# Three reorderings around the attention chains of a two-block transformer kernel on one Trainium2 core

## The chip, the core and the metric

The kernel runs on one core of one Trainium2 chip. The metric is the device time of one execution in microseconds (us). Before the change three executions took 1301.56, 1304.0 and 1314.62 us; the median is 1304.0 us. TensorE (PE) does the matmuls, VectorE (DVE) and ScalarE (ACT) work between them on PSUM and SBUF, GpSimd (POOL) makes one half of each split weight, and SyncE (SP) issues the weight stream.

## The reference, cut to what matters

All inputs are float32, the sequence has 256 tokens and the model width is 1024. A first block has windowed attention and a bidirectional mLSTM, a gated merge and a convolutional feed-forward layer. A second model of two layers follows: its first mixer has eight "forgetting" heads (fox) and eight "stick-breaking" heads (sb), its second a short convolution, and each is followed by a feed-forward layer. The fox heads and the output product are what most of the change is about:

```python
def forgetting_attention(q, k, v, log_f):
    cum_f = jnp.cumsum(log_f, axis=-1)
    ...
        logits = jnp.einsum('bhqd,bhkd->bhqk', qi, k,
                            preferred_element_type=jnp.float32) * scale
        logits = logits + fi[..., :, None] - cum_f[:, :, None, :]
        logits = jnp.where(causal, logits, -jnp.inf)
        p = jax.nn.softmax(logits, axis=-1)
        return jnp.einsum('bhqk,bhkd->bhqd', p.astype(v.dtype), v)
...
    o = jnp.concatenate([o_fox, o_sb], axis=1)
    o = o.transpose(0, 2, 1, 3).reshape(b, s, MIX_WIDTH)
    return o @ w_out
```

The other place is the first block's attention, where the gate `gm` is one of the input projections and the softmax runs over latent keys, context keys and a sink.

## The kernel before

**Weights.** Every 128x1024 weight block is loaded by SP into `raw`, rounded by ACT into `whi` (line 1146, `splits_upto`), and the remainder is made by POOL into `wlo` (line 313). A product is three matmuls, high by high, high by low and low by high (lines 482 to 484, `mm3`). The three buffers are rings of six blocks, so a block's ACT split waits until the block six places earlier has been used up (`blk_done`).

**Order.** Each engine has one hand-written program. Nothing is scheduled by a planner; the order of the Python loops is the order on the engine, and semaphores tie the engines together.

**First attention.** TensorE goes through 16 steps `st`. A step has the scores (`att_scores`, lines 770 and 774), in eight of the steps one `gm` projection of 24 matmuls (`gp_job`, steps 1, 3, 5, 7, 9, 11, 15 and 16, from the table `GM_AT`), the transposes of the step before (`att_transposes`, line 785), and in odd steps the values and reciprocals of a pair (`att_values` line 796, `att_recips` line 807). All `gm` projections write the same PSUM bank, so each of them waits until ACT has evacuated the one before (`evac`, line 1238, which also makes the next weight's split). On ACT a step is: `evac` of the projection of step `st - 1`, then the two exponentials of step `st` (lines 1325 and 1327), then in even steps the copy of the reciprocals (line 1334), for which a DVE multiply waits (line 1895).

**Fox chain.** For head h the chain is

- `fox_scores(h)` on TensorE: eight matmuls, lines 1010 to 1016, into one of two banks
- `fox_maximum(h)` on DVE: two reductions, line 2120
- `fox_exps(h)` on ACT: two exponentials, line 1468
- `fox_even(h)` on DVE: reciprocal and two scalings, lines 2126 and 2129
- `fox_transposes(h)` on TensorE: three transposes, line 1028, which wait for `fox_even(h)`
- `fox_turned(h)` on DVE: copy out of PSUM, line 2137
- `fox_values(b)` on TensorE for two heads: lines 1037 and 1041 (the sb heads have `sb_values`, lines 988 and 992)
- `out_hi`, `out_lo` on ACT (line 1459) and DVE (line 2113): the split of the pair's output for the last product

`scores(h)` waits for the exponentials of head h - 2, since there are two score banks. On TensorE iteration h holds `fox_transposes(h - 2)`, `fox_scores(h)`, in the first two iterations `sb_values(3)` and the products that spread the norms (`spread_rstd`, line 924), for h from 4 to 7 one half of an output product (`out_half(h - 4, 0)`, twelve matmuls of lines 482 to 484), and for even h from 4 a `fox_values`.

The output product of eight blocks accumulates in eight PSUM regions. For blocks 0 to 3 it is cut into two halves, `out_half(n, 0)` for the first four regions and `out_half(n, 1)` for the rest. A first half may start as soon as the norms of all queries and keys are done, a second one only when all fox exponentials are done, because its banks hold the scores. Blocks 4 and 5 (`product_k`) and the pair 6 and 7 follow whole.

On DVE the last pass of the projection loop (`j == 17`) and the lines behind it are `fox_maximum(0)`, `finish_qk(10)`, `sb_exponents(7)`, `fox_even(0)`, `sb_masked(7)`, `finish_qk(11)`, `row_rstd(3)` (four short operations, lines 1578 to 1582), `fox_maximum(1)`. After that iteration h is `fox_turned(h - 2)`, `fox_even(h - 1)`, `fox_maximum(h)`, with h = 2 as an exception that puts the maximum first. On ACT pass 17 is `fox_exps(0)`, `row_rsqrt(3)` (lines 1432 and 1435), `sb_weights(7)` (line 1454), `out_hi(2)`.

Of the kernel before, what the change touches and what calls it, by code (L numbers as in the profile page):

```python
# [36 lines left out]
GM0 = W_IN_JOBS.index("gm")  # L37
# [88 lines left out]
def build(nc, xc_d, ccol_d, params_d, const_d, const1_d, const2_d, wgate_d, wf_d, stream_d, out_d):  # L126
# [3 lines left out]
    with ctx:  # L130
# [349 lines left out]
        def _(pe):  # L480
# [565 lines left out]
            def out_half(n, half):  # L1046

                wait_rest(pe, S_OUT2 + n)
                pe.wait_ge(S["t2_lo"], n + 1)
                if half == 0:  # L1050
                    pe.wait_ge(S["qk_fin"], 26)
                else:
                    pe.wait_ge(S["fox_exp"], 16)
                for m in range(4 * half, 4 * half + 4):
                    mm = mm3(PS[:, m // 2, (m % 2) * T:(m % 2) * T + T], *w(S_OUT2 + n, m), *out_rows(n),
                             n == 0 and m % 2 == 0, False)
                if half == 1:
                    mm.then_inc(blk_done, 1)
# [24 lines left out]
            for h in range(2, 11):  # L1083
                if h < 10:
                    fox_transposes(h - 2)
                if h < 8:
                    fox_scores(h)
                if h == 2:
                    sb_values(3)
                if h in (2, 3):  # L1090
                    spread_rstd(2 * h + 8)
                    spread_rstd(2 * h + 9)
                if 4 <= h < 8:
                    out_half(h - 4, 0)
                if h in (8, 9):
                    out_half(h - 8, 1)
                if h in (4, 6, 8, 10):
                    fox_values((h - 4) // 2)
            for n in (2, 3):
                out_half(n, 1)  # L1100
            for n in (4, 5):
                wait_rest(pe, S_OUT2 + n)
# [30 lines left out]
        def _(act):  # L1133
# [180 lines left out]


            for st in range(STEPS + 3):
                if st - 1 in GM_AT:
                    evac(GM0 + GM_AT[st - 1])
                if st < STEPS:
                    for half in range(2):  # L1320
                        u = 2 * st + half
                        act.wait_ge(S["att_max"], u + 1)
                        if u >= 4:
                            act.wait_ge(S["tr_done"], u - 3)
                        act.activation(a_P[u % 4], PS[:, SCORE_BANKS[st % 2][half], :], ACT.Exp, bias=nmx[:, u:u + 1],
                                       accum_out=rsum[:, u:u + 1]).then_inc(S["att_exp"], 1)
                        act.activation(esk[:, u:u + 1], nmx[:, u:u + 1], ACT.Exp, bias=pr("sink", u, u + 1))\
                           .then_inc(S["sink_act"], 1)
                if st % 2 == 0 and st >= 4:
                    b = (st - 4) // 2  # L1330
                    act.wait_ge(S["recip_bc"], b + 1)
                    if b >= 1:
                        act.wait_ge(S["att_out"], b)
                    act.activation(a_R, PS[:, 6, T:2 * T], ACT.Copy).then_inc(S["recip_out"], 1)
# [116 lines left out]
            def sb_weights(h):  # L1451

                act.wait_ge(S["sb_arg"], h + 1)
                act.activation(sbW[h % 4], sbW[h % 4], ACT.Exp).then_inc(S["sb_w"], 1)
# [16 lines left out]
            for j in range(18):  # L1471
                if j == 17:
                    fox_exps(0)
                if j in (5, 9, 13, 17):
                    g = (j - 5) // 4
                    if g >= 1:
                        act.wait_ge(S["rq_done"], 2 + g)
                    row_rsqrt(g)
                if j == 17:
                    sb_weights(7)  # L1480
                if 0 <= j - 9 < 8:
                    sb_logs(j - 9)
                if 0 <= j - 10 < 7:
                    sb_weights(j - 10)
                if j in (13, 15, 17):
                    out_hi((j - 13) // 2)
                if j < 16:
                    act.wait_ge(blk_done, S_ATT2 + KC + j + 1)
                    if 6 <= j < 14:
                        act.wait_ge(S["fin_bc"], j - 5)  # L1490
                    if j >= 2:
                        act.wait_ge(S["st_done"], 10 + j - 1)
                    act.activation(sqr2[j % 2], PS[:, 4 + j % 2, 0:T], ACT.Square).then_inc(S["qk_sq"], 1)
                    if j == 4:
                        act.wait_ge(S["f_add"], 1)
                        act.activation(fr[1][0:8, :], fr[0][0:8, :], ACT.Abs).then_inc(S["f_act"], 1)
                        act.wait_ge(S["f_act"], 1)
                        act.activation(fr[1][0:8, :], fr[1][0:8, :], ACT.Exp, scale=-1.0).then_inc(S["f_act"], 1)
                        act.wait_ge(S["f_act"], 2)
                        act.activation(fr[1][0:8, :], fr[1][0:8, :], ACT.Ln, bias=1.0).then_inc(S["f_act"], 1)  # L1500
                    splits_upto(S_ATT2 + KC + j + RING)
# [40 lines left out]
        def _(dve):  # L1542
# [600 lines left out]
            for j in range(18):  # L2143
                if j in (5, 9, 13):
                    row_rstd((j - 5) // 4)
                if j == 6:
                    forget_sums()
                if j == 17:
                    fox_maximum(0)
                if 7 <= j:  # L2150
                    finish_qk(j - 7)
                if 0 <= j - 10 < 8:
                    sb_exponents(j - 10)
                if 0 <= j - 9 < 8:
                    sb_terms(j - 9)
                if j == 17:
                    fox_even(0)
                if 0 <= j - 10 < 8:
                    sb_masked(j - 10)
                if j in (13, 15):  # L2160
                    out_lo((j - 13) // 2)
                if j < 16:
                    dve.wait_ge(S["qk_sq"], 10 + j + 1)
                    dve.tensor_copy(q2[:, j, :], PS[:, 4 + j % 2, 0:T]).then_inc(S["evac_v"], 1)
                if j == 3:
                    dve.wait_ge(S["gates2_ps"], 1)
                    dve.tensor_scalar(fr[0][0:8, :], PS[0:8, 7, 0:T], pr("fb", rows=slice(0, 8)), None, ALU.add)\
                       .then_inc(S["f_add"], 1)
# [1 line left out]

            finish_qk(11)
            row_rstd(3)
            fox_maximum(1)
            for h in range(2, 12):
                if h < 10:
                    fox_turned(h - 2)
                if h == 2:
                    fox_maximum(h)
                    out_lo(2)
                if h < 9:  # L2180
                    fox_even(h - 1)
                if 3 <= h < 8:
                    fox_maximum(h)
                if h in (2, 3):
                    finish_qk(2 * h + 8)
                    finish_qk(2 * h + 9)
# [209 lines left out]
```

## Time and profile before

| | us |
|---|---|
| median of three executions | 1304.0 (1301.56 to 1314.62) |
| the profiled execution | 1304.0 |
| its span, first to last instruction | 1302.2 |
| TensorE busy in it | 1256.8 |
| mean granted TensorE clock | 0.984 of full speed |

The page gives one execution. Its busy times say how long an engine had work in flight; its chain says what ended last; its timeline gives the start and the duration of every instruction. Matmuls are pipelined, so a row's duration is longer than the distance to the next row's start, and the distance is what the engine's time costs. The granted clock is given for any stretch: 1.00 is 2.4 GHz and 0.50 is 1.2 GHz.

### The profile page before, as it was taken

To read this page: it belongs to the slowest core of one execution; us is meant where nothing else is said; L and a number is where in the kernel's file an instruction comes from. 1 tells how busy PE (TensorE), PEld (TensorE's weight loads), DVE (VectorE), ACT (ScalarE), POOL (GpSimd) and SP (SyncE) were. 2 spreads that over 40 slices of the span, in tenths; PEclk is the share of its full clock that TensorE was granted. 3 is DMA by queue.
4 is the path that set the end of the run, shared out by engine and by line. 5 is a ranking of instruction groups with operands and counts; after the bars stand their busy time and mean duration, and the time that the engine had idled before them with its cause. 6 is when DMAs were issued, how large, how long until landed. Compare 5 with 4: busy or idle time off the path is not lost.

```text
span 1302.2 us, 24847 instructions
## 1 busy us (share of the span) xinstructions
PE 1256.8 (97%) x9248; PEld 1150.0 (88%) x9248; DVE 784.6 (60%) x1432; ACT 628.6 (48%) x1081; POOL 700.2 (54%) x299
## 2 busy tenths in 40 slices
PE   5789999999999899999899999999999999999998
PEld 1578888877799799999888778999999999999998
DVE  3699467536631477766555663677776424677775
ACT  3523233445443555555544543655455545645553
POOL 1546563252148555557585312655566886755564
PEclk9899999999999899999999989999999999999999
DMA  9568662141125445545453211455446555445552
GB/s 376 205 218 304 222 210 68 63 129 51 49 91 167 132 147 192 193 174 215 154 178 114 82 49 51 144 194 186 171 176 211 164 186 169 156 169 192 193 188 72
DMA packets 57739, 208.45 MB, mean 160 GB/s; under 512 B 6576, under 2 KB 7600, under 8 KB 57408
## 3 DMA queue, kind: packets, MB, share of 16 engines
q1 hardware_dynamic: 57168, 205.55, 46.2%
q0 software_dynamic: 496, 1.87, 0.4%
q8 instruction: 50, 0.82, 0.3%
q14 instruction: 25, 0.20, 0.1%
HBM read 206.35 MB, written 1.05 MB: 159 GB/s over the span
## 4 chain that ended last, share of the span: by engine, by line
PE 89%; DVE 6%; DMA 3%; issue 1%; ACT 1%; SPq 0%; DVEq 0%; ACTq 0%
PE ps L482 24%; PE ps L483 23%; PE ps L484 23%; DMA raw<-in_stream 3%; PE ps L703 2%; PE ps L517 2%; PE ps L519 2%; PE ps L520 2%; PE ps L547 1%; PE ps L770 1%; PE ps L796 1%; PE ps L785 1%; DVE raw L1647 1%; PE ps L924 1%; PE ps L1016 1%
## 5 line engine op out<-in xcount | busy, mean ns | idle before, releaser
L313 POOL TENSOR_TENSOR wlo<-raw,whi 128x1024 fp32r<-128x1024 f32 x286 | 694.4, 2444 | 564.0 <-ACT whi L1146 539.6
L482 PE MATMUL ps<-Hh,whi 128*128 128x256 f32 (+2 forms) x1976 | 578.2, 293 | 15.8 <-DVE Hl L1613 4.7
L483 PE MATMUL ps<-Hl,whi 128*128 128x256 f32 (+2 forms) x1976 | 569.1, 288 | 0.0
L484 PE MATMUL ps<-Hh,wlo 128*128 128x256 f32 (+2 forms) x1976 | 568.8, 288 | 0.0
L482 PEld LDWEIGHTS ps<-Hh,whi 128*128 128x128 f32 (+1 forms) x1976 | 382.2, 193 | 30.2 <-issue 16.6
L1146 ACT ACTIVATE whi<-raw 128x1024 fp32r<-128x1024 f32 x338 | 352.9, 1052 | 111.7 <-DMA raw<-in_stream 56.1
L483 PEld LDWEIGHTS ps<-Hl,whi 128*128 128x128 f32 (+1 forms) x1976 | 382.8, 194 | 3.0
L484 PEld LDWEIGHTS ps<-Hh,wlo 128*128 128x128 f32 (+1 forms) x1976 | 382.5, 194 | 2.6
L2002 DVE SCALAR_TENSOR_TENSOR arena<-ps,sm,arena 128x255 f32<-128x255 f32 (+1 forms) x264 | 127.3, 482 | 102.7 <-ACT arena L1396 94.8
L482 PE MATMUL ps<-dh,whi 128*128 128x256 f32 x592 | 167.7, 283 | 1.5 <-DVE dl L1914 1.1
L483 PE MATMUL ps<-dl,whi 128*128 128x256 f32 x592 | 167.5, 283 | 0.0
L484 PE MATMUL ps<-dh,wlo 128*128 128x256 f32 x592 | 167.5, 283 | 0.0
L1396 ACT ACTIVATE arena<-ps,sm 128x256 f32<-128x256 f32 x132 | 66.5, 504 | 133.2 <-DVE ps L1992 104.3
L482 PEld LDWEIGHTS ps<-dh,whi 128*128 128x128 f32 x592 | 113.6, 192 | 1.9 <-issue 1.3
L484 PEld LDWEIGHTS ps<-dh,wlo 128*128 128x128 f32 x592 | 113.7, 192 | 0.0
L483 PEld LDWEIGHTS ps<-dl,whi 128*128 128x128 f32 x592 | 113.7, 192 | 0.0
L1964 DVE COPY sm<-params 128x8 f32 (+1 forms) x66 | 89.9, 1367 | 7.9 <-DVE arena L2002 7.6
L1975 DVE TENSOR_TENSOR wlo<-raw,whi 128x1024 fp32r<-128x1024 f32 x52 | 81.2, 1562 | 1.5
L1407 ACT ACTIVATE dh<-ps 128x256 fp32r<-128x256 f32 x60 | 23.0, 384 | 101.3 <-DVE ps L2011 101.3
L1647 DVE SCALAR_TENSOR_TENSOR raw<-raw,arena 128x1024 f32<-128x1024 f32 x32 | 56.4, 1792 | 4.4 <-DMA raw<-in_stream 4.2
L517 PE MATMUL ps<-whi,Hh 128*128 128x512 f32 (+1 forms) x128 | 48.0, 375 | 4.0 <-DVE Hl L1634 4.0
L519 PE MATMUL ps<-whi,Hl 128*128 128x512 f32 (+1 forms) x128 | 47.5, 371 | 0.0
(298 smaller groups left out, 1230.1 us busy)
## 6 DMA issues: line engine op xcount, KB each, us to landing
raw<-in_stream SPq DMA_DIRECT2D x386, 512.0 KB, 4.1
X<-in_xc SPq DMA_DIRECT2D x2, 1024.0 KB, 10.1
out_y<-X SPq DMA_DIRECT2D x8, 128.0 KB, 2.0
kx<-in_const POOLq DMA_DIRECT2D x1, 512.0 KB, 6.9
arena<-in_wgate POOLq DMA_DIRECT2D x1, 400.0 KB, 8.8
params<-in_params POOLq DMA_DIRECT2D x1, 372.0 KB, 6.8
k<-in_const POOLq DMA_DIRECT2D x1, 256.0 KB, 4.5
kx<-in_const POOLq DMA_DIRECT2D x1, 256.0 KB, 4.5
```

The costliest lines, as they stand in the source:

```text
L313: pool.tensor_tensor(wlo[:, slot, :], raw[:, rslot, :], whi[:, slot, :].bitcast(f32), ALU.subtract).then_inc(rest_done[0], 1)
L482: pe.matmul(out, lh, rh, start=start, stop=False, skip_group_check=True)
L483: pe.matmul(out, lh, rl, start=False, stop=False, skip_group_check=True)
L484: return pe.matmul(out, ll, rh, start=False, stop=stop, skip_group_check=True)
L517: pe.matmul(out, Hh[:, k, tok], wh_, start=k == 0 and first, stop=False, skip_group_check=True)
L519: pe.matmul(out, Hl[:, k, tok], wh_, start=False, stop=False, skip_group_check=True)
L1146: act.activation(whi[:, s % RING, :], raw[:, r % RING, :], ACT.Copy).then_inc(hi_done, 1)
L1396: act.activation(tc, PS[:, 4 + 2 * slot + j, 0:T], ACT.Identity, bias=bias, scale=cwb[:, slot, 3 * j:3 * j + 1]).then_inc(S["centre"], 1)
L1647: dve.scalar_tensor_tensor(raw[:, r % RING, :], raw[:, r % RING, :], 1.0, c_across, ALU.mult, ALU.mult, accum_out=MODB[:, at:at + 1]).then ...
L1964: dve.tensor_copy(cwb[:, i % 2, :], src).then_inc(S["cw_copy"], 1)
L1975: dve.tensor_tensor(wlo[:, s % RING, :], raw[:, RAW_OF_W[s] % RING, :], whi[:, s % RING, :].bitcast(f32), ALU.subtract).then_inc(rest_done ...
L2002: dve.scalar_tensor_tensor(tc[:, lo:hi], u[:, src:src + hi - lo], cwb[:, slot, 3 * j + 1 + n:3 * j + 2 + n], tc[:, lo:hi], ALU.mult, ALU.a ...
```

## The change

It has four parts, and no arithmetic changes.

1. First attention, ACT: `evac` of a `gm` projection moves from before the exponentials of the next step to behind them.
2. Projection loop, pass 17: on ACT `sb_weights(7)` moves ahead of `row_rsqrt(3)`. On DVE `fox_even(0)` leaves this pass, and `out_lo(2)` enters it at its end.
3. Fox loop on DVE: it now starts at h = 1, and the maximum of head h stands ahead of `fox_even(h - 1)` in every iteration; `fox_even(0)` comes behind `fox_maximum(1)`.
4. Fox loop on TensorE: the four `out_half(n, 0)` leave iterations 4 to 7. Two of them stand in iteration 8 and two in iteration 9, and all four `out_half(n, 1)` follow the loop. A first half now waits for the split outputs of all four sb pairs (`t2_lo` of 4).

```diff
                 wait_rest(pe, S_OUT2 + n)
-                pe.wait_ge(S["t2_lo"], n + 1)
                 if half == 0:
+                    pe.wait_ge(S["t2_lo"], 4)
                     pe.wait_ge(S["qk_fin"], 26)
...
-                if 4 <= h < 8:
-                    out_half(h - 4, 0)
                 if h in (8, 9):
-                    out_half(h - 8, 1)
+                    out_half(2 * h - 16, 0)
+                    out_half(2 * h - 15, 0)
                 if h in (4, 6, 8, 10):
                     fox_values((h - 4) // 2)
-            for n in (2, 3):
+            for n in range(4):
                 out_half(n, 1)
...
             for st in range(STEPS + 3):
-                if st - 1 in GM_AT:
-                    evac(GM0 + GM_AT[st - 1])
                 if st < STEPS:
...
+                if st - 1 in GM_AT:
+                    evac(GM0 + GM_AT[st - 1])
...
                 if j == 17:
                     fox_exps(0)
+                    sb_weights(7)
...
                     row_rsqrt(g)
-                if j == 17:
-                    sb_weights(7)
...
-                if j == 17:
-                    fox_even(0)
                 if 0 <= j - 10 < 8:
                     sb_masked(j - 10)
-                if j in (13, 15):
+                if j in (13, 15, 17):
                     out_lo((j - 13) // 2)
...
-            fox_maximum(1)
-            for h in range(2, 12):
-                if h < 10:
+            for h in range(1, 12):
+                if 2 <= h < 10:
                     fox_turned(h - 2)
-                if h == 2:
+                if h < 8:
                     fox_maximum(h)
-                    out_lo(2)
-                if h < 9:
+                if 1 <= h < 9:
                     fox_even(h - 1)
-                if 3 <= h < 8:
-                    fox_maximum(h)
```

**ACT in the first attention.** Before, from the exponentials of an odd step (lines 1325 and 1327) over the evacuation (1238) and the split (1146) to those of the next even step and the copy of the reciprocals (1334):

```order
L1325 ACTIVATE arena,sm<-ps,sm 128x512
L1327 ACTIVATE sm<-sm,params 128x1
L1238 ACTIVATE arena<-ps 128x256
L1146 ACTIVATE whi<-raw 128x1024
L1325 ACTIVATE arena,sm<-ps,sm 128x512
L1327 ACTIVATE sm<-sm,params 128x1
L1325 ACTIVATE arena,sm<-ps,sm 128x512
L1327 ACTIVATE sm<-sm,params 128x1
L1334 ACTIVATE arena<-ps 128x256
```

Now the same instructions have the lines 1322, 1324, 1237, 1145 and 1333, and in the same place stands:

```order
L1322 ACTIVATE arena,sm<-ps,sm 128x512
L1324 ACTIVATE sm<-sm,params 128x1
L1322 ACTIVATE arena,sm<-ps,sm 128x512
L1324 ACTIVATE sm<-sm,params 128x1
L1237 ACTIVATE arena<-ps 128x256
L1145 ACTIVATE whi<-raw 128x1024
L1333 ACTIVATE arena<-ps 128x256
```

The evacuation and the split stand behind the exponentials of the even step instead of in front of them.

**DVE around `row_rstd(3)`.** Before, from `sb_exponents(7)` (line 2101) over `fox_even(0)` (2126 and twice 2129), `sb_masked(7)` (2107), `finish_qk(11)` (2053) and `row_rstd(3)` to `fox_maximum(1)` (2120):

```order
L2101 TENSOR_TENSOR arena<-arena,ps 128x384
L2126 RECIPROCAL sm<-sm 128x2
L2129 TENSOR_SCALAR arena<-arena,sm 128x128
L2129 TENSOR_SCALAR arena<-arena,sm 128x256
L2107 TENSOR_TENSOR arena<-arena,kx 128x384
L2053 SCALAR_TENSOR_TENSOR arena<-arena,params,ps 128x256
L1578 TENSOR_SCALAR arena<-ps 8x256
L1580 SCALAR_TENSOR_TENSOR arena<-arena 8x256
L1581 TENSOR_TENSOR arena<-arena 8x256
L1582 SCALAR_TENSOR_TENSOR arena<-arena 8x256
L2120 TENSOR_REDUCE sm<-ps 128x1 x2
L2137 COPY arena<-ps 128x384
```

Now, with all lines two lower:

```order
L2099 TENSOR_TENSOR arena<-arena,ps 128x384
L2105 TENSOR_TENSOR arena<-arena,kx 128x384
L2111 TENSOR_TENSOR Hl<-ps,Hh 128x256
L2051 SCALAR_TENSOR_TENSOR arena<-arena,params,ps 128x256
L1576 TENSOR_SCALAR arena<-ps 8x256
L1578 SCALAR_TENSOR_TENSOR arena<-arena 8x256
L1579 TENSOR_TENSOR arena<-arena 8x256
L1580 SCALAR_TENSOR_TENSOR arena<-arena 8x256
L2118 TENSOR_REDUCE sm<-ps 128x1 x2
L2124 RECIPROCAL sm<-sm 128x2
L2127 TENSOR_SCALAR arena<-arena,sm 128x128
L2127 TENSOR_SCALAR arena<-arena,sm 128x256
```

`fox_even(0)` (2124, 2127) has moved behind `row_rstd(3)` and the maximum of head 1, and `out_lo(2)` (2111) stands ahead of `finish_qk(11)` and `row_rstd(3)`.

**TensorE behind the scores of head 5.** Before, their last two matmuls (lines 1014 and 1016) are followed by `out_half(1, 0)`, of whose twelve matmuls the first three are shown:

```order
L1014 MATMUL ps<-Hh 128x128
L1016 MATMUL ps<-arena 128x256
L482 MATMUL ps<-Hh,whi 128x256
L483 MATMUL ps<-Hl,whi 128x256
L484 MATMUL ps<-Hh,wlo 128x256
```

Now the transposes of head 4 (line 1028) and the scores of head 6 follow at once:

```order
L1014 MATMUL ps<-Hh 128x128
L1016 MATMUL ps<-arena 128x256
L1028 MATMUL ps<-k,arena 128x128 x3
L1010 MATMUL ps<-Hh 128x128
L1012 MATMUL ps<-Hh 128x128
```

The twelve matmuls that stood between scores and transposes are behind the chain.

## Rows read from the trace of the kernel before

**Rows 1.** The page: span, busiest engine, POOL's group (busy, mean ns | idle)
```profile
span 1302.2 us, 24847 instructions
PE 1256.8 (97%) x9248; PEld 1150.0 (88%) x9248; DVE 784.6 (60%) x1432; ACT 628.6 (48%) x1081; POOL 700.2 (54%) x299
...
L313 POOL TENSOR_TENSOR wlo<-raw,whi 128x1024 fp32r<-128x1024 f32 x286 | 694.4, 2444 | 564.0 <-ACT whi L1146 539.6
```

**Rows 2.** Timeline of ACT, first attention, steps 3 to 4: start, duration, [idle]
```profile
303.16 0.39 ACT L1238 ACTIVATE arena<-ps 128x256 f32<-128x256 f32 x1
...
308.46 0.69 ACT L1325 ACTIVATE arena<-ps,sm 128x512 f32<-128x512 f32 x1 [3.97 <-DVE rows L1872]
...
310.17 0.38 ACT L1334 ACTIVATE arena<-ps 128x256 f32<-128x256 f32 x1
```

**Rows 3.** Timeline of PE: first matmul of the `gm` projection of step 5
```profile
309.90 0.33 PE L482 MATMUL ps<-Hh,whi 128*128 128x256 f32 x1
```

**Rows 4.** Timeline of PE, fox chain: heads 2 and 3, then 4 and 5
```profile
767.20 0.55 PE L1028 MATMUL ps<-k,arena 128*128 128x128 f32 x3
767.50 0.31 PE L1010 MATMUL ps<-Hh 128*128 128x128 f32 x1
...
769.49 0.65 PE L988 MATMUL ps<-arena 128*64 128x256 f32 x4
...
770.29 1.13 PE L924 MATMUL ps<-arena,kx 8*128 8x256 f32 x4
...
775.52 0.46 PE L1010 MATMUL ps<-Hh 128*128 128x128 f32 x1
...
779.03 0.58 PE L482 MATMUL ps<-Hh,whi 128*128 128x256 f32 x1
...
781.89 1.12 PE L1037 MATMUL ps<-arena 128*64 128x256 f32 x4
...
783.37 0.90 PE L1028 MATMUL ps<-k,arena 128*128 128x128 f32 x3
783.92 0.46 PE L1010 MATMUL ps<-Hh 128*128 128x128 f32 x1
```

**Rows 5.** Windows of the fox chain: length, busy time (instructions) by engine, PEclk
```profile
core 0: us, PE busy (x) PEld busy (x) DVE busy (x) ACT busy (x) POOL busy (x), PEclk, DMA share, GB/s
765.00:770.00 5.00, 5.00 (x35) 3.50 (x33) 4.02 (x12) 1.30 (x5) 0.00 (x0) 1.00 0.01 3
770.00:775.00 5.00, 5.00 (x28) 3.17 (x24) 4.17 (x14) 1.52 (x7) 0.00 (x0) 0.94 0.01 2
775.00:780.00 5.00, 5.00 (x18) 3.89 (x18) 2.61 (x8) 0.79 (x4) 0.00 (x0) 0.50 0.00 0
780.00:785.00 5.00, 5.00 (x26) 3.98 (x24) 0.66 (x3) 0.71 (x4) 0.00 (x0) 0.54 0.00 0
785.00:790.00 5.00, 5.00 (x33) 3.89 (x31) 2.66 (x9) 1.19 (x5) 0.00 (x0) 1.00 0.00 0
```

**Rows 6.** Timeline of DVE around `row_rstd(3)`, and heads 4 and 3 later
```profile
765.50 0.47 DVE L2053 SCALAR_TENSOR_TENSOR arena<-arena,params,ps 128x256 f32<-128x256 f32 x1
765.89 0.40 DVE L1578 TENSOR_SCALAR arena<-ps 8x256 f32<-8x256 f32 x1
...
767.67 0.62 DVE L2120 TENSOR_REDUCE sm<-ps 128x1 f32<-128x128 f32 x2
...
779.14 0.62 DVE L2120 TENSOR_REDUCE sm<-ps 128x1 f32<-128x128 f32 x2 [1.98 <-PE ps L1016]
...
784.78 0.16 DVE L2126 RECIPROCAL sm<-sm 128x2 f32<-128x2 f32 x1
784.98 0.55 DVE L2129 TENSOR_SCALAR arena<-arena,sm 128x128 f32<-128x128 f32 x2
```

**Rows 7.** Timeline of ACT, pass 17 of the projection loop
```profile
763.64 0.45 ACT L1432 ACTIVATE arena<-ps,sm 8x256 f32<-8x256 f32 x1
...
764.46 0.53 ACT L1454 ACTIVATE arena<-arena 128x384 f32<-128x384 f32 x1
765.31 0.38 ACT L1459 ACTIVATE Hh<-ps 128x256 fp32r<-128x256 f32 x1 [0.32 <-PE ps L992]
```

## The prediction

> **What bounds the kernel now.** I read the page first: TensorE is busy for 1256.8 us of a span of 1302.2 [rows 1], so only two things can lengthen or shorten this kernel, time in which TensorE waits and time in which its clock is low. Then I read the timelines of the two places that the change touches and asked of each who is late. In the first attention TensorE runs without a gap, and ACT is the one that waits: 3.97 us before the exponentials of step 4 [rows 2]. In the fox chain TensorE is again busy 5.00 us of every 5.00, while DVE waits up to 1.98 us for scores [rows 5, 6]. So before the change both chains are bound by TensorE, and the latency of DVE and ACT is covered by matmuls that lie between a head's scores and its transposes. The windows show a second thing. The granted clock is 1.00 up to 770, mixed in the next window and 0.50 in 775 to 780, and it is back at 1.00 in 785 to 790 [rows 5]. The low stretch is (1 - 0.94) x 5 / 0.5 = 0.6, plus 5.0, plus (1 - 0.54) x 5 / 0.5 = 4.6, together 10.2 us, so the clock falls near 774.4 and returns near 784.6. TensorE was at its full 2.4 GHz with the busy row full when it fell to 1.2 GHz; what ran just before were matmuls of few rows (line 924 uses 8 of 128) and scores, and the weight-load row was only 3.17 of 5.00.
>
> **Unit costs.** From starts of neighbouring rows [rows 4]: scores take 769.49 - 767.50 = 1.99 us at full clock and 779.03 - 775.52 = 3.51 at half; transposes 0.30 and 0.55; a pair of values 770.29 - 769.49 = 0.80 and 783.37 - 781.89 = 1.48; twelve matmuls of an output half 2.86 at half clock. Half clock thus makes a piece 1.76 to 1.85 times as long, and I use 1.8. From the end of a head's scores the way back to its transposes is, if DVE does maximum and scaling in a row: 0.11 to the maximum (779.03 to 779.14), 0.62 for it, 0.03 between, 784.98 + 0.55 - 784.78 = 0.75 for reciprocal and scalings, and 0.1 back to TensorE (taken like the way out): 1.6 us [rows 4, 6].
>
> **Part 1, the evacuation.** A `gm` projection waits for the evacuation of the one before. Before, that sits at 303.16 and the next projection starts at 309.90, with 6 us in hand [rows 2, 3]. Now it comes behind the exponentials of the even step. These end where the copy of the reciprocals starts, at 310.17; the evacuation takes 0.39, and with 0.05 for the semaphore the projection starts at 310.6 instead of 309.90: 0.7 us late. This applies to steps 3, 5, 7, 9 and 11; the projections of steps 15 and 16 wait for one that is long done or whose ACT neighbourhood has no exponentials. The exponentials follow the scores at a fixed distance, so the lag does not grow: 5 x 0.7 = 3.5 us. Behind the moved evacuation are queued the split (one block, needed about five projections later, so hidden by the ring of six), the copy of the reciprocals and through it DVE's maximum of the odd step, some 1.4 us late; TensorE needs those exponentials only after the projection, transposes, values and the next scores, over 6 us, so they stay hidden. Bounds: 0 if ACT is a little earlier than this, 5 if the lag of DVE also reaches TensorE. I take 3.5.
>
> **Parts 2 and 3, before head 2.** In program order TensorE has transposes 0 right behind scores 1, at 767.20 [rows 4]. Now they wait for `fox_even(0)`, which DVE has behind `out_lo(2)`, `finish_qk(11)`, `row_rstd(3)` and `fox_maximum(1)`. ACT: `sb_weights(7)` cannot start before 764.46, as before; the two operations of `row_rsqrt(3)` now follow it, to 765.85, and `out_hi(2)` ends at 766.25, where it started at 765.31 before [rows 7]. DVE then does `out_lo(2)` (0.4, to 766.65), `finish_qk(11)` (0.39 by its distance to the next row, to 767.05), `row_rstd(3)` (767.67 - 765.89 = 1.78, to 768.8), the maximum (0.62) and `fox_even(0)` (0.75): 770.15, and TensorE goes on at 770.25 [rows 6]. Its gap is 3.05 us. Of that 1.1 come from the swap and the moved `out_lo(2)`; without them it would be 1.95. Nothing fills the gap, since scores 2 stand behind these transposes.
>
> **Parts 3 and 4, heads 2 to 7.** Transposes h - 1 now wait 1.6 us from the end of scores h, since maximum h stands ahead of `fox_even(h - 1)`. What TensorE has in between: for heads 2 and 3 the sb values and the line 924 products (1.1 us or more a pair), for even heads from 4 a pair of values, for heads 5 and 7 nothing. So after scores 5 and 7 it waits 1.6 each, 3.2 together. After scores 4 and 6 it waits 0.1 at half clock or 0.8 at full, after scores 3 nothing or 0.5. At half clock that is 0.25 in all.
>
> **Part 4, the clock.** The 48 moved matmuls are no new work, but they were the densest thing in the chain. Before, the clock came back 5.6 us after `out_half(0, 0)` began at 779.03. Now a gap of 3 us precedes head 2 and no dense product comes before iteration 8. I take it that the clock falls at about 771 and stays at 1.2 GHz until 5.6 us into the output halves. Cost at half clock: six scores 6 x 1.52 = 9.1, less 0.3 for a first piece at full clock; transposes 1 to 6, 6 x 0.25 = 1.5; three pairs of values 3 x 0.68 = 2.0; two pairs of line 924 products, estimated 0.5 each, 1.0; the output halves 5.6 x (1 - 1/1.8) = 2.5. Together 15.8. What the low stretch of before cost, 10.2 x (1 - 1/1.8) = 4.5, is in the old time already, so 11.3 are added. Bounds: -4.5 if the clock never falls, 13 if it comes back late.
>
> **Costed at nothing.** The second halves of blocks 0 to 3 finish later, so ACT's splits of blocks 6 and on wait about 1 us more; the whole products 4 and 5, twice as long as a half, and four halves ahead of them cover one split and POOL's 2.44 us [rows 1]. If that cover failed it would cost 1 to 2 us. The wait on `t2_lo` of 4 is met since iteration 3.
>
> **Sum.** 3.5 + 3.05 + 3.2 + 0.25 + 11.3 = 21.3. The profiled execution took 1304.0 us, the median too: 1325.
>
> **The Trainium skill on the clock.** "TensorE: Matmul & The Clock Gate", section "Why this matters for your kernels", lets the clock fall after TensorE has stood idle between bursts of matmuls. In this trace it fell with the busy row at 5.00 of 5.00 [rows 5], so the trace disagrees with that as the only cause. By the rule alone, the gaps of 1.6 us would do less than I forecast; it is the second rival's ground.
>
> **Rivals.** (a) The clock returns inside the chain, where values and transposes stand together behind scores 4. For: such a mixture, with a few output matmuls, ran just before 784.6. Against: scores at half clock follow at once and TensorE did not recover on them between 775 and 779. It would save three scores, three transposes, one pair of values and the tail, 4.6 + 0.75 + 0.7 + 2.5, less 0.7 for a wait that half clock had covered: 7.8, giving 1317.5. (b) The clock follows idle time rather than density and the fall is no longer than before, or absent. Then the waits are those at full clock, 3.05 + 3.2 + 0.5 + 0.8 + 0.8 = 8.35, and the time is 1304.0 + 3.5 + 8.35 = 1316, or 1311.5 with no fall at all. Against: two waits of 1.6 us make the chain thinner than the one on which it fell. (c) Not slower: `fox_even(0)` is ready when scores 1 end, and putting the maximum first lets heads follow each other while the output halves, now in one dense run, keep the clock up. It decides at transposes 0: if they start within 0.3 us of the end of scores 1, the 4.5 us of low clock are saved and the time is 1299.5. Against: in the new order `fox_even(0)` cannot even start before the maximum of head 1, which needs the end of those scores. (d) The evacuation does nothing: 1321.5, inside my own range.
>
> **How the numbers follow.** Forecast 0.66, (a) 0.15, (b) 0.15, (c) 0.04. The forecast's own range is 1318 to 1332: 3.5 less at the bottom for (d), 3 for the clock, and 7 on top for late recovery, the lag of DVE and the cover of the splits. Taking in (a) and most of (b) gives 1310 to 1332. One per cent of 1304.0 is 13.0 us, about what a measurement of this kernel can tell from no change. Slower than 1317.0: nearly all of the forecast (0.63), half of (a) (0.08) and 0.01 of (b): 0.72. Faster than 1291.0: no case gives it, 0.03 for the unforeseen. Within: 0.25.
>
> **What would show it.** Right: waits of TensorE on line 1237 of about 0.7 us, five times; a gap of about 3 us before the first transposes (now line 1028 waiting on DVE 2127) and two of 1.6; a clock of 0.50 from about 774 to 815 of the new trace. The clock row decides between forecast, (a) and (b): the same gaps with a clock of 1.00 give 1311 to 1316. I would be wrong at the root if transposes did not wait on DVE at all, or if the clock stayed up over the 3 us gap.

## The result and the profile after

The changed kernel takes 1327.95 us (median of 4 executions, 1326.45 to 1329.60); beside it the kernel before took 1303.22. The ratio is 1.0162 with a 95% interval of 1.0124 to 1.0201: slower by 1.6%. That ratio is not the quotient of the two medians, which are 24.7 us or 1.9% apart; on 1303.22 us it is 21.1 us, with 16.2 to 26.2 as its interval. One execution of the kernel before that is on record beside the last experiments, 1530.08 us at a mean clock of 0.747, is in no number below. The profiled execution took 1325.02 us. These are its lines that answer to the page of before [rows 1]:

```profile
span 1323.2 us, 24847 instructions
PE 1266.8 (96%) x9248; PEld 1155.2 (87%) x9248; DVE 785.6 (59%) x1432; ACT 629.3 (48%) x1081; POOL 701.9 (53%) x299
```

The instruction counts are the same on every engine. The span is 21.0 us longer and TensorE is busy 10.0 us longer with the same 9248 matmuls, so about half of the loss is work that runs more slowly and the rest is waiting. Which waits, the chain of semaphores tells: the view of waits for TensorE over the whole span (engine, line, releaser: us in total, times, longest):

```profile
PE ps L1028 <- DVE arena L2127: 5.4, 3, 2.7
...
PE ps L482 <- ACT arena L1237: 4.3, 7, 1.1
...
PE ps L796 <- DVE arena L1893: 1.4, 1, 1.4
```

The first is the fox chain, the other two hold the first attention (the second has two waits elsewhere; within 296 to 362 us it shows 2.7 us in 5). The kernel before shows none of these three in those stretches. A projection starts 0.7 to 0.75 us late where the profile counts 0.54 of waiting, since it counts from the modelled end of the row before.

**First attention.** ACT after, to be read against [rows 2], with lines 3 lower for the exponentials:

```profile
299.67 0.69 ACT L1322 ACTIVATE arena<-ps,sm 128x512 f32<-128x512 f32 x1 [3.12 <-DVE rows L1870]
...
301.38 0.38 ACT L1237 ACTIVATE arena<-ps 128x256 f32<-128x256 f32 x1
301.64 1.06 ACT L1145 ACTIVATE whi<-raw 128x1024 fp32r<-128x1024 f32 x1
```

And TensorE, two of the five projections, and the values of step 13 [rows 3]:

```profile
301.81 0.39 PE L482 MATMUL ps<-Hh,whi 128*128 128x256 f32 x1 [0.54 <-ACT arena L1237]
...
312.42 0.39 PE L482 MATMUL ps<-Hh,whi 128*128 128x256 f32 x1 [0.53 <-ACT arena L1237]
...
356.71 1.95 PE L796 MATMUL ps<-arena 128*64 128x256 f32 x16 [1.37 <-DVE arena L1893]
```

ACT idles 3.12 us and then makes the evacuation last, at 301.38, and the projection starts right behind it. From one projection to the next is now 312.42 - 301.81 = 10.61 us.

**Fox chain.** TensorE after, against [rows 4]:

```profile
774.98 0.55 PE L1028 MATMUL ps<-k,arena 128*128 128x128 f32 x3 [2.67 <-DVE arena L2127]
775.28 0.31 PE L1010 MATMUL ps<-Hh 128*128 128x128 f32 x1
...
780.08 2.07 PE L924 MATMUL ps<-arena,kx 8*128 8x256 f32 x4
...
782.08 0.90 PE L1028 MATMUL ps<-k,arena 128*128 128x128 f32 x3
...
799.20 0.90 PE L1028 MATMUL ps<-k,arena 128*128 128x128 f32 x3 [1.37 <-DVE arena L2127]
...
810.26 0.90 PE L1028 MATMUL ps<-k,arena 128*128 128x128 f32 x3 [1.37 <-DVE arena L2127]
810.81 0.56 PE L482 MATMUL ps<-Hh,whi 128*128 128x256 f32 x1
```

The row at 810.81 is the first matmul of an output half. On DVE after, what TensorE waits for at 774.98 [rows 6]:

```profile
771.13 0.42 DVE L2111 TENSOR_TENSOR Hl<-ps,Hh 128x256 fp32r<-128x256 f32 x1 [0.51 <-ACT Hh L1458]
...
773.64 0.62 DVE L2118 TENSOR_REDUCE sm<-ps 128x1 f32<-128x128 f32 x2
774.18 0.15 DVE L2124 RECIPROCAL sm<-sm 128x2 f32<-128x2 f32 x1
774.37 0.55 DVE L2127 TENSOR_SCALAR arena<-arena,sm 128x128 f32<-128x128 f32 x2
```

And the windows, with the clock, against [rows 5]:

```profile
770.00:775.00 5.00, 2.33 (x17) 1.50 (x13) 4.18 (x12) 1.77 (x7) 0.00 (x0) 1.00 0.00 0
775.00:780.00 5.00, 5.00 (x21) 3.25 (x21) 1.80 (x6) 0.85 (x5) 0.00 (x0) 0.55 0.02 5
780.00:785.00 5.00, 5.00 (x18) 3.63 (x16) 1.52 (x3) 0.28 (x2) 0.00 (x0) 0.50 0.00 0
...
805.00:810.00 5.00, 3.89 (x13) 2.71 (x12) 1.60 (x6) 0.42 (x3) 0.00 (x0) 0.50 0.00 0
810.00:815.00 5.00, 4.74 (x29) 4.61 (x31) 1.78 (x6) 0.77 (x4) 0.00 (x0) 0.70 0.00 0
815.00:820.00 5.00, 5.00 (x45) 4.24 (x43) 0.89 (x2) 0.49 (x2) 0.00 (x0) 1.00 0.01 3
```

The column behind POOL is the granted clock. A window of 5 us at a clock c holds (1 - c) x 10 us at 1.2 GHz: 4.5, six windows of 5.0 from 780 to 810, and 3.0, together 37.5 us from 775.5 to 813.0. Before it was 10.2.

**Where the 21 us are.** I compared the starts of the same work in both traces. At the start of the first attention the new trace is 1.1 us behind, at its end 6.0: about 5.0 us. At the start of the fox chain it is only 5.0 behind, since the low stretches elsewhere in the execution fell differently: outside the chain the trace of before has 30.7 us at 1.2 GHz, the new one 23.9. From the start of the chain to the end of the span it loses 16.0. In the chain the three waits are 5.4. Of the 37.5 us at low clock 2.7 are waiting (the two waits of 1.37), which a clock does not lengthen; so 34.8 - 10.2 = 24.6 us more of work at 1.2 GHz, at 1 - 1/1.8 = 0.44 each, are 10.9. Together 16.3, against 16.0 found.

### The profile page after: what moved, and what is told of

The parts are those of the page before. It is cut to its first block, busy times and chain, and to the rows that moved or that the text cites. A ratio compares the mean times of both kernels' runs of the same rounds, so it can differ in the third digit from the quotient of the medians.

```text
span 1323.2 us, 24847 instructions
## 1 busy us (share of the span) xinstructions
PE 1266.8 (96%) x9248; PEld 1155.2 (87%) x9248; DVE 785.6 (59%) x1432; ACT 629.3 (48%) x1081; POOL 701.9 (53%) x299
## 3 DMA queue, kind: packets, MB, share of 16 engines
HBM read 206.35 MB, written 1.05 MB: 157 GB/s over the span
## 4 chain that ended last, share of the span: by engine, by line
PE 88%; DVE 6%; DMA 3%; issue 2%; ACT 2%; SPq 0%; DVEq 0%; ACTq 0%
PE ps L482 24%; PE ps L483 23%; PE ps L484 23%; DMA raw<-in_stream 3%; PE ps L703 2%; PE ps L517 2%; PE ps L519 2%; PE ps L520 2%; PE ps L547 1%; PE ps L796 1%; PE ps L1016 1%; PE ps L770 1%; DVE raw L1645 1%; PE ps L924 1%; PE ps L785 1%
## 6 DMA issues: line engine op xcount, KB each, us to landing
X<-in_xc SPq DMA_DIRECT2D x2, 1024.0 KB, 10.4
```

## The experiments

Eleven kernels ran besides the two. Two theories of the clock stood against each other in them: by the first it falls and stays low when TensorE stands idle, by the second when its work is thin. "Dense" here is a run of matmuls that all use 128 rows and 256 columns, as in an output half; "thin" is the mixture of the chain, where many have 8 or 64 rows or 128 columns. "Low" is the length of the stretch at 1.2 GHz in the fox chain, added up from the windows as above; "waits" is what TensorE waits there for DVE; "reckoned" is what the last section's arithmetic makes of both, 5.0 us for part 1, and the fill's own time (waits inside the low stretch are not counted twice). "Clock" is the mean granted clock of a whole execution, averaged over the timed executions (their number behind it); it counts every low stretch and not only that of the chain. One thousandth of it is 2.6 us at 1.2 GHz, about 1.2 us of time.

| kernel | median us | ratio to before (95%) | waits | low | measured - before | reckoned | clock |
|---|---|---|---|---|---|---|---|
| changed kernel | 1327.95 | 1.0162 (1.0124 to 1.0201) | 5.4 | 37.5 | 24.7 | 21.3 | 0.9722 (4) |
| part 1 alone | 1309.69 | 1.0047 (1.0030 to 1.0064) | 0 | 10.3 | 6.3 | 5.0 | 0.9848 (6) |
| part 4 alone | 1309.90 | 1.0042 (1.0007 to 1.0078) | 0 | 23.9 | 6.5 | 6.1 | 0.9780 (5) |
| parts 2 and 3 | 1313.02 | 1.0072 (1.0052 to 1.0092) | 2.7 | 23.9 | 9.6 | 8.4 | 0.9782 (4) |
| part 3 alone | 1309.54 | 1.0053 (1.0033 to 1.0073) | 1.7 | 20.5 | 5.9 | 6.3 | 0.9818 (4) |
| parts 1 to 3 | 1317.59 | 1.0099 (1.0063 to 1.0135) | 2.7 | 20.4 | 13.0 | 12.2 | 0.9810 (4) |
| changed, `fox_even(0)` back | 1318.60 | 1.0123 (1.0104 to 1.0143) | 2.7 | 27.3 | 15.0 | 14.1 | 0.9770 (4) |
| changed, gaps filled | 1317.68 | 1.0110 (1.0085 to 1.0136) | 0.8 | 13.7 | 14.3 | | 0.9832 (4) |
| before, dense fill | 1303.39 | 1.0005 (0.9983 to 1.0026) | 0 | 0 | -0.2 | -1.6 | 0.9856 (12) |
| before, fill of 8 rows | 1308.85 | 1.0048 (1.0029 to 1.0066) | 0 | 13.7 | 5.3 | 3.5 | 0.9821 (9) |
| before, short dense fill | 1301.95 | 0.9997 (0.9962 to 1.0032) | 0 | 0 | -2.7 | -3.6 | 0.9848 (12) |
| before, half moved forward | 1308.26 | 1.0020 (0.9999 to 1.0041) | 0 | 23.9 | 3.6 | 6.1 | 0.9817 (12) |

The medians of before beside them were 1303.42 us (mean clock 0.9846 of 10 executions) for part 1, part 4, parts 2 and 3 together, and the filled gaps; 1303.60 (0.9847 of 20) for part 3, `fox_even(0)` back, the dense fill and the fill of 8 rows; and 1304.63 (0.9838 of 22) for parts 1 to 3, the short fill and the moved half. The ratios are not quotients of these medians: for parts 1 to 3 the ratio is worth 12.9 us, for the moved half 2.6, for the short fill -0.4.

**Part 1 alone**, in the kernel before:

```diff
-                if st - 1 in GM_AT:
-                    evac(GM0 + GM_AT[st - 1])
                 if st < STEPS:
...
+                if st - 1 in GM_AT:
+                    evac(GM0 + GM_AT[st - 1])
```

> The kernel before with part 1 alone (evacuation behind the exponentials). Theory: the lag of ACT reaches TensorE five times (about 0.75 us a period in the trace after) and DVE's lag once more at the values of step 13 (about 1.2 us): +5.0 us, 4.5 to 5.5. As the prediction had it, five times 0.7 and nothing at step 13: +3.5. Rival, evacuation hidden: 0.

The waits of TensorE from 296 to 362 us:

```profile
PE ps L482 <- ACT arena L1238: 2.7, 5, 0.5
PE ps L796 <- DVE arena L1895: 1.4, 1, 1.4
```

Six lags, not five: five projections and the values of step 13. Part 1 costs 0.47% by itself, 3.9 to 8.3 us by its interval, which holds the 5.0 expected; the median difference of 6.3 lies above the stated 5.5. In the changed kernel the waits are the same.

**Part 4 alone**: the four `out_half(n, 0)` leave the chain of the kernel before. The edit is cut here; the wait on `t2_lo` and the loop behind the chain change as in the whole change.

```diff
-                if 4 <= h < 8:
-                    out_half(h - 4, 0)
                 if h in (8, 9):
-                    out_half(h - 8, 1)
+                    out_half(2 * h - 16, 0)
+                    out_half(2 * h - 15, 0)
```

> The kernel before with part 4 alone (output halves behind the chain, DVE and ACT as before). No transposes wait for DVE in this order. Theory (the clock follows how dense the work is): it falls near 774 as before, and without the output halves it comes back only when they begin, 22 to 26 us of half clock instead of 10.2: +5 to +7 us. Rival (the clock falls only after idle time): no wait is added, so no longer low stretch: 0 us, -1 to +1.

Four windows of TensorE's busy time and clock:

```profile
770.00:775.00 5.00, 5.00 (x29) 3.37 (x29) 4.33 (x15) 1.13 (x5) 0.00 (x0) 0.98 0.01 2
775.00:780.00 5.00, 5.00 (x18) 3.38 (x19) 2.73 (x9) 0.97 (x5) 0.00 (x0) 0.50 0.00 0
...
790.00:795.00 5.00, 5.00 (x21) 3.56 (x18) 1.52 (x6) 0.68 (x4) 0.00 (x0) 0.50 0.00 0
795.00:800.00 5.00, 5.00 (x31) 4.79 (x31) 1.78 (x6) 1.19 (x5) 0.00 (x0) 0.63 0.01 3
```

Busy is 5.00 of 5.00 in all of them and no wait on DVE exists, yet the clock is down for 23.9 us instead of 10.2. This is the cleanest separation of density from idle time: moving 48 dense matmuls out of the chain keeps the clock low without a single gap. It is not an accident of one profile, since the five executions have a mean clock of 0.9780 against 0.9846.

The end of the low stretch is the steady part. The clock came back 3.6 us behind the start of the first output half here (795.10 to 798.7), 5.6 in the kernel before, and 2.2 in the changed kernel. In all eleven profiles with a low stretch in the chain it came back 2.2 to 5.6 us behind the first dense piece that followed the fall, and in none before it.

**Parts 2 and 3, and part 3 alone.** The first has the new order of DVE and of pass 17 and TensorE as before; in the second `sb_weights(7)` and `out_lo(2)` are where they were, too. Two places of the edit:

```diff
-                if j == 17:
-                    fox_even(0)
...
-                if j in (13, 15):
+                if j in (13, 15, 17):
                     out_lo((j - 13) // 2)
```

The last two changed lines are in the first kernel alone.

> The kernel before with parts 2 and 3 alone (orders of DVE and ACT in the fox chain; the output halves keep their place). Theory: one gap of about 2.7 us before the first transposes, the later waits of 1.6 us lie under the output halves; the clock falls at or before 775 and comes back within the halves, 10 to 14 us low: +3 to +5 us. Rival (the whole effect of the fox chain comes from DVE's order): +14 to +16 us.

> The kernel before with DVE's order of the fox loop alone (part 3), without the swap on ACT and without the moved out_lo(2). As the prediction split it: the gap before the first transposes is 1.1 us shorter than with part 2 (1.6 to 1.95 instead of 2.7), the clock falls at the same place, 0.8 to 1.2 us less than e3. Rival (part 2 costs nothing): same gap and time as e3, 1313.

The wait before the first transposes, read from TensorE's timeline, is 2.67 us in the first. In the second:

```profile
768.33 0.79 PE L1028 MATMUL ps<-k,arena 128*128 128x128 f32 x3 [1.73 <-DVE arena L2129]
```

So part 2 costs 2.67 - 1.73 = 0.94 us of waiting, which is what was expected of it, and a low stretch 3.4 us longer. Both times missed their expectations by the low clock. Parts 2 and 3 cost 9.6 us and not 3 to 5: the wait is of the size expected, but the stretch is 13.7 us longer than before. Part 3 alone came out 3.5 us below them and not 0.8 to 1.2. The four executions of parts 2 and 3 have clocks of 0.975 to 0.982, mean 0.9782, against 0.9846 for before, so the longer stretch is theirs in general.

**Parts 1 to 3**: the changed kernel with TensorE's output halves where they were before.

> The changed kernel with part 4 undone: the output halves stand in the chain again. If the three parts simply add up (part 1 6.1, parts 2 and 3 9.4, in their own runs), 1319 us; low stretch beginning within a step of 770 to 776 and ending within about 6 us of the start of the output halves, so 17 to 27 us long instead of 37.6; no wait of 1.4 us on DVE in the chain, only the first one of about 2.7. Rival (the waits, not the missing density, make the low stretch long): it stays above 30 us and the time above 1324.

```profile
775.24 0.55 PE L1028 MATMUL ps<-k,arena 128*128 128x128 f32 x3 [2.67 <-DVE arena L2128]
```

```profile
775.00:780.00 5.00, 4.76 (x21) 3.28 (x21) 1.74 (x7) 0.85 (x6) 0.00 (x0) 0.58 0.02 3
...
790.00:795.00 5.00, 5.00 (x19) 4.01 (x19) 1.24 (x5) 0.91 (x4) 0.00 (x0) 0.50 0.00 0
795.00:800.00 5.00, 5.00 (x32) 3.63 (x32) 1.56 (x6) 0.39 (x3) 0.00 (x0) 0.88 0.00 0
```

The first fence is the one wait that is left, the second the windows: the clock is back 1.2 us into the window from 795, 3.7 us behind the start of the first output half at 792.47. With the halves in the chain the two waits of 1.37 vanish (they cover DVE's answer again) and the low stretch is 17 us shorter. Part 4 is worth 1327.95 - 1317.59 = 10.4 us here, where it cost 6.5 in the kernel before; by the two ratios it is 8.2, with each kernel's own before beside it 11.7. The arithmetic gives 2.7 for the waits and, since these lie inside the low stretch, (17.1 - 2.7) x 0.44 = 6.4, together 9.1. The rival, that waits alone make the stretch long, asked for over 30 us and falls.

**Changed kernel with `fox_even(0)` back in pass 17**, which takes the first wait away and leaves parts 1 and 4:

```diff
+                if j == 17:
+                    fox_even(0)
...
-                if 1 <= h < 9:
+                if 2 <= h < 9:
                     fox_even(h - 1)
```

> The changed kernel with fox_even(0) back in pass 17, so that the first transposes wait for nothing. Theory: the 2.7 us gap goes, the fall of the clock comes one group of products later, and the rest of the low stretch stays since it is the lack of output halves that holds it: 3 to 5 us less than the changed kernel, 1322 to 1325, low stretch 30 to 36 us. Rival (the gap is what brings the clock down): low stretch as short as before, 1310 to 1313.

It came out between the two and missed both ranges of the theory, for the time and for the stretch: 1318.60, 9.4 us below the changed kernel. Only the two waits of 1.37 are left. The low stretch is 27.3 us, 10.2 shorter, since the fall came at 779.4 in place of 775.5 and the output halves, which end it, began at 803.63 in place of 810.81. With 2.7 for the wait and 10.2 x 0.44 = 4.5 this reckons 7.2.

**Changed kernel with the gaps filled.** Products of 128 rows into a score bank whose contents are used up stand before transposes 0 (20 of them) and before those of heads 4 and 6 (10 each). Nobody reads what they write, and the output is the same.

```diff
+                if h in (2, 6, 8):
+                    filler(20 if h == 2 else 10, h)
                 if h < 10:
                     fox_transposes(h - 2)
```

> The changed kernel with matmuls that compute nothing of use in its gaps (20 before the first transposes, 10 before those of heads 4 and 6). Rival (idle time decides the clock): with the gaps filled it stays up or is low for no longer than in the kernel before, 1312 to 1318 us. Theory (density decides): the fall comes at the products that spread the norms as in the kernel before, and scores with 10 extra matmuls at half clock are still too thin to bring it back: 1326 to 1331 us.

```profile
780.00:785.00 5.00, 4.79 (x24) 3.58 (x23) 3.71 (x12) 1.19 (x5) 0.00 (x0) 0.82 0.00 0
785.00:790.00 5.00, 5.00 (x21) 3.18 (x20) 1.55 (x6) 0.91 (x4) 0.00 (x0) 0.50 0.00 0
790.00:795.00 5.00, 5.00 (x19) 3.89 (x18) 1.80 (x6) 0.84 (x5) 0.00 (x0) 0.50 0.00 0
795.00:800.00 5.00, 4.43 (x27) 3.43 (x25) 2.22 (x7) 1.08 (x6) 0.00 (x0) 0.81 0.00 0
```

Doing more work makes it 10 us faster. The number lies where the idle theory had it, but the run does not speak for idle time: with the large gap gone the clock still fell, at 783.2, among the 8-row products of head 3 (782.34 to 783.57), where the only wait near it is one of 0.21 us that starts behind the fall. It returned at 796.9, behind the ten dense products that began at 793.40, and stayed up for the rest of the chain. My density theory was wrong in expecting that so few dense products would not bring it back.

**The kernel before with a fill beside the 8-row products.** Sixteen products stand among the `spread_rstd` of heads 2 and 3; once with 128 rows, once with 8 rows and otherwise the same.

```diff
                     spread_rstd(2 * h + 8)
+                    filler(4, h + 1)
                     spread_rstd(2 * h + 9)
+                    filler(4, h + 1)
```

> The kernel before with 16 dense matmuls (128 rows, 256 columns) that compute nothing of use beside the eight products that spread the last norms. Theory (density decides): the fall near 774 does not come; 1.9 us of extra work against 4.5 us saved, -2 to -3 us. Rival (it falls whatever stands there): +1.9 us. A low stretch of 0 near 774 decides.

> As e6, with the same 16 extra matmuls using 8 rows instead of 128, for the same time on the engine. Theory, if it is filled rows that count: the clock falls as in the kernel before and the work is extra, +1.5 to +2.5 us. Rival, if streamed columns count: as e6, -2 to -3 us.

With 128 rows:

```profile
770.00:775.00 5.00, 5.00 (x33) 3.50 (x31) 3.40 (x12) 0.91 (x4) 0.00 (x0) 1.00 0.02 5
775.00:780.00 5.00, 5.00 (x28) 3.53 (x28) 3.33 (x10) 1.19 (x5) 0.00 (x0) 1.00 0.00 0
780.00:785.00 5.00, 5.00 (x35) 3.78 (x34) 1.80 (x6) 0.92 (x4) 0.00 (x0) 1.00 0.00 0
```

With 8 rows:

```profile
775.00:780.00 5.00, 5.00 (x28) 3.91 (x26) 3.21 (x10) 0.68 (x4) 0.00 (x0) 0.87 0.02 5
780.00:785.00 5.00, 5.00 (x20) 4.18 (x18) 2.48 (x7) 1.00 (x5) 0.00 (x0) 0.50 0.00 0
785.00:790.00 5.00, 5.00 (x19) 3.98 (x21) 0.62 (x2) 0.91 (x4) 0.00 (x0) 0.50 0.00 0
```

Number, columns and place of the matmuls are the same, and TensorE is busy throughout in both. Only the rows in use differ, and with them the time: eight of 128 rows add 1.45 us at full clock by the starts of the rows around them, eight of 8 rows 0.95. In the profiles the dense kernel's clock never fell in the chain and the thin one's fell for 13.7 us. The executions agree: the medians are 5.5 us apart with intervals that do not meet, and the mean clocks are 0.9856 and 0.9821. The thin fill cost 5.3 us, more than the 1.5 to 2.5 expected.

The dense fill gained nothing, where 2 to 3 us were expected. Its own 2.9 us are one reason. The other is that the clock of its executions, 0.9856, is hardly above the 0.9847 of before: some 2 us less at 1.2 GHz and not 10.2. Its profile shows how: 0 in the chain, but 40.8 us elsewhere, where the profile of before has 30.7. That the fill kept the clock up against the kernel before is thus seen in one profile and not shown over its executions; that 128 rows hold it better than 8 is.

**A shorter fill, and a useful one.** Three dense products behind the `spread_rstd` of heads 2 and 3 in place of eight; and, in another kernel, `out_half(0, 0)` between the transposes of head 2 and the scores of head 4.

> The kernel before with 6 dummy products of 128 rows (3 behind the spread products of heads 2 and 3 each) in place of the 16 of the dense fill. They cost 12 x 0.11 at most, about 0.7 us at full clock. If this little density is enough to keep the clock at 1.00, the time is 4.5 - 0.7, some 3 to 4 us below before, 1299 to 1301; if it is not, low stretch as before and 0.5 to 1 us above before. Both keep all of TensorE's waits at nothing.

> The kernel before with one useful dense piece moved forward: out_half(0, 0) stands between the transposes of head 2 and the scores of head 4, instead of behind those scores. Theory (thin work brings the clock down and keeps it down, dense work brings it back): the fall comes as before, near 774 us, since what lies ahead of it is unchanged; the dense piece comes 3.5 us earlier, so the low stretch is 6.8 or 10.2 us long, not more, and the time is 0 to 2 us below before. Rival (position does not matter, the stretch has a fixed course): same as before within 0.5 us, low stretch of 10.2 us.

The short fill's profile shows a clock of 1.00 through the chain, with transposes 2 and 3 at full clock, and its median is the lowest of all, but 3 of its 12 executions took 1315 us, the interval runs from 0.38% faster to 0.32% slower, and its mean clock of 0.9848 is hardly above the 0.9838 of before. A gain is not shown. The moved half missed both expectations: it was not faster, its low stretch is 23.9 us long, and its windows say something about all single profiles:

```profile
765.00:770.00 5.00, 5.00 (x19) 3.18 (x19) 3.44 (x10) 1.05 (x3) 0.00 (x0) 0.50 0.02 3
```

Here the clock fell at 764.0, ten us earlier than in the trace of before, with the same instructions ahead of it. The end was as elsewhere: the moved half began at 785.23 and the clock was back at 787.9. So the place of the fall is not fixed by the program alone. One profile's start of the low stretch carries no proof; that the stretch began at 770.2 with parts 2 and 3, and at 768.5 with part 3, may be such a shift in part, though the mean clocks say that these kernels do run longer at 1.2 GHz.

## Why the prediction was right

1325 us was forecast, 1327.95 measured, and the range of 1310 to 1332 holds it. Both halves of the argument stand: TensorE's own waits and its clock.

- **Part 1, 3.5 us forecast, 5.0 found.** The mechanism is the forecast one. Two sizes were off. Each lag is 10.61 - 9.86 = 0.75 us and not 0.7, where 9.86 is their distance before (300.04 to 309.90). And the step "TensorE needs those exponentials only after the projection, transposes, values and the next scores, over 6 us" fails at step 13, which has no projection. There DVE's multiply (line 1893) waits 1.29 us for the copy of the reciprocals, queued behind the 1.06 us split, and the values of step 13 wait 1.37 for the multiply; 1.2 us are lost. The forecast's upper bound of 5, "if the lag of DVE also reaches TensorE", was this case. Rival (d), no effect, falls with part 1 alone.
- **Before head 2, 3.05 forecast, 2.67 found**, on the releaser named. `out_lo(2)` to the end of `fox_even(0)` ran as in the forecast's list; the list added durations where the rows overlap. From `sb_weights(7)` to `out_hi(2)` ACT takes 1.23 us from start to start (769.51 to 770.74) and not 1.39, and the maximum 0.54 (773.64 to 774.18) and not 0.62. Its share of the swap and `out_lo(2)` was given as 1.1 and is 0.94.
- **After scores 5 and 7, 3.2 forecast, 2.7 found.** Twice 1.37 in place of 1.6. After scores 3, 4 and 6 nothing was found for the 0.25.
- **The clock, 11.3 forecast, 10.9 found**, with two errors against each other. The fall was where the forecast had it: 0.75 us behind the first transposes (771 and 770.25 on the times of before), and measured 0.5 behind them (775.5 and 774.98 on those of the new trace). But the clock came back 813.0 - 810.81 = 2.2 us into the output halves where I had taken 5.6 from the trace of before, which costs 1.0 us and not 2.5. On the other side a group of line 924 products costs 2.00 us at half clock (780.08 to 782.08) where it took 1.05 before at full (770.29 to 771.34), so 0.95 more each and not the estimated 0.5. That the fall came as forecast has luck in it, since its place moves between profiles.
- **The rivals.** (a) had the clock back inside the chain; the windows stay at 0.50 up to 810. (b) had it follow idle time; part 4 alone shows 23.9 us of low clock with none. (c) needed transposes 0 within 0.3 us of scores 1; they came 2.67 behind.
- **The sum** was 21.3, and what was found adds up to 5.0 + 5.4 + 10.9 = 21.3 again. That they agree to the tenth is luck: 1.5 too little for part 1 stands against 1.1 too much for the waits and 0.4 for the clock. The spans differ by 21.0. The medians differ by 24.7; the profiled execution of the changed kernel is 2.9 us below its median, that of before within 1 us of its. The granted clocks go the same way: 0.977 in the profiled execution, 0.971 to 0.973 in the four timed ones, so these spent some 13 us more at 1.2 GHz. At 0.44 that is more than enough for the 2.9; where in the kernel it lay no trace shows.

The Trainium skill's rule in "TensorE: Matmul & The Clock Gate", section "Why this matters for your kernels", has the clock fall after idle gaps between bursts. The trace of before has such a fall too, at 37.1 us, long before the chains, while TensorE stands idle:

```profile
36.00:38.00 2.00, 0.00 (x0) 0.00 (x0) 1.96 (x2) 0.78 (x2) 2.00 (x2) 0.77 1.03 410
38.00:40.00 2.00, 0.00 (x0) 0.00 (x0) 1.89 (x5) 2.00 (x5) 1.99 (x1) 0.50 1.03 408
```

Against it as the only cause stand part 4 alone and the 8-row fill: 23.9 and 13.7 us at 1.2 GHz with the busy row at 5.00 of 5.00. A gap is one way to lose the clock; thin matmuls are another.

What stays open: how the wait of 2.67 us lengthens the low stretch. Parts 2 and 3 had 23.9 us of it, against 10.2 before, with the halves in place, and the clocks of their four executions say the same. TensorE's own program is that of before there, so the wait is the likely cause. But the stretch also began early in that profile, and by how much the wait moves the fall is not shown.

## What to carry to other kernels

Where TensorE sets the time, ask of every matmul that is moved not only what it covers but what clock it holds up: 48 matmuls that were merely moved cost 6.5 us with no wait at all, and about 10 in the company of waits that they had covered. When two engines hand each other work, walk the whole loop for the step that lacks the usual filler (here step 13) before a lag is called hidden. And compare medians and the mean clocks of many executions before trusting where a single trace shows the clock fall, or that it does not: a low stretch that is gone from one place may stand in another.

## What the runs showed of the hardware

- The granted clock fell to 1.2 GHz while TensorE was continuously busy (5.00 of 5.00 us), and the rows in use count: with 16 matmuls of 128 rows it stayed at 1.00 in the chain, with 16 of 8 rows in the same places it fell for 13.7 us. Over 12 and 9 executions the mean clocks were 0.9856 and 0.9821.
- Thin work did not bring it back: in part 4 alone it stayed at 0.50 from 775 to 795 with TensorE busy throughout.
- It came back within 2.2 us of dense output halves in the changed kernel, and after ten dense products in a chain that stayed thin otherwise (796.9, 3.5 us behind their start). Over all eleven profiles with a low stretch in the chain the delay was 2.2 to 5.6 us.
- The fall's place moves from one execution to another by some 10 us with the same program ahead of it: 774.4 in the kernel before, 764.0 with the half moved forward. The low stretches outside the chain vary as well, from 23.9 us (changed kernel) to 40.8 (dense fill) in the profiles.
- At half clock the four 8-row products took 2.0 us by the next row's start (780.08 to 782.08), against 1.05 at full (770.29 to 771.34 before).
